# Self-attention's mean squares of the heads' outputs: from ScalarE, head by head, to GpSimd, token tile by token tile

## The chip, the cores and the metric

The kernel runs on one core of one Trainium2 chip. The metric is the time of one execution on the device in microseconds, the median of several runs; lower is better.

## The reference

One decoder layer for 1024 tokens of width 1024, in float32. Ahead of the change stands an input projection and a Mamba-2 mixer; the change is in differential attention, four heads of 128 outputs each:

```python
    p = jax.nn.softmax(s, axis=-1)
    attn = p[:, :, 0] - lam * p[:, :, 1]
    return jnp.einsum('bhqk,bhkv->bhqv', attn.astype(v.dtype), v)
...
    o = rms_norm(o, subln_w) * (1.0 - lambda_init)     # mean of o*o over the 128 outputs of a head
```

Behind it come the output projection, cross-attention into 256 memory tokens, and an MLP. What the change concerns is, for every token and head, the sum of the squares of the 128 outputs `o`, from which `rms_norm` takes its scale.

## The kernel before, in words

All engines run programs of their own, written out in order, and meet at semaphores; each engine works strictly through its own order. Float32 products are made as three products of high and low parts on TensorE (`three`), so most matrices are split: ScalarE makes the high part (`split_hi`, `tr_hi`), VectorE the low part (`split_lo`, `tr_lo`).

**Attention** runs over 32 steps, one for each pair of a query tile i (128 tokens) and a head h. Their order is `ATT_STEPS` (line 183): query tiles in pairs, 7 and 3, 6 and 2, 5 and 1, 4 and 0, the four heads of a pair alternating between its two tiles; tile i has (i + 1) * 128 keys. In step n the engines do, each at its own place in its loop:

- TensorE: two score matrices (L2277, with the mask L2281), the transposes of the combined probabilities of an earlier step (L2296), the product with the values of step n - 3 (L2315) into PSUM bank 7. That product waits for `o_ev` of the step before it, since the bank must be free.
- VectorE: the two maxima (`attn_max`, L1609), and between them the combination of the two softmaxes of step n - 1 (`attn_comb`, L1618, L1619, L1621); `attn_comb` waits for `o_ev` of four steps ago before it overwrites the reciprocals.
- ScalarE: the copy of the transposed probabilities (L1003), the output of step n - 3 taken from PSUM twice, once as a scaled copy into `mix` (L1018) and once as a scaled square with its sum in `stat` (L1023), and the two exponentials (L986).
- GpSimd: next to nothing; it makes the powers of -1/2 for all norms of the kernel, one for each entry of `POWS` (line 199), in that order (`pow_step`, L752).

For the norm of a tile VectorE first scales the four sums to means (`o_mean`, L1626, its instruction is in the helper `mean`, L1338), GpSimd raises them to -1/2, and VectorE multiplies `mix` by the result (`o_norm`, L1631). In VectorE's loop of 39 iterations the mean of a tile stands at the end of the iteration six after the step of its last head (`O_STEP`), the multiplication in the iteration after that, ahead of the mean of the pair's other tile:

```python
                if n - 7 in O_COMPLETE:
                    o_norm(O_COMPLETE[n - 7])
                if n - 6 in O_COMPLETE:
                    o_mean(O_COMPLETE[n - 6])
```

ScalarE copies the last head of that tile in the iteration three after its step. `MIX_TILES` (line 194) is the order in which tiles are complete: 7, 3, 6, 2, 5, 1, 4, 0. In iterations beyond 32 VectorE makes the low parts of the memory tokens, and the means and multiplications of tiles 4 and 0.

**Behind attention** TensorE makes the memory's keys and values in 16 steps (line 2327), two for each unit of weights. The weights pass through two slots: SyncE loads a raw half when the half two before it is split (`load_half` waits for `w_lo`), ScalarE makes its high part (L820), VectorE its low part (L1334), and TensorE waits for both halves' low parts at the first step of a unit (`unit_ready`). After every second step TensorE transposes one tile of `mix` (L2139). In VectorE's order the first of these low parts stand behind the multiplication of tile 0.

Of the kernel before, what the change touches and what calls it, by code (L numbers as in the profile page):

```python
# [27 lines left out]
ALU = mybir.AluOpType  # L28
ACT = mybir.ActivationFunctionType
AX = mybir.AxisListType  # L30

P = 128
T = 1024
D = 1024
NT = T // P
# [6 lines left out]
DH = 4  # L42
# [169 lines left out]
COL, N_COLS = {}, 0  # L212
# [7 lines left out]
def build(nc, t, out):  # L220
    ctx = ExitStack()
    with ctx:
# [10 lines left out]
        def at(name, region, offset, shape, dt=F32):  # L233
            return nc.alloc_sbuf_tensor_at(name, shape, dt, offset=place[region] + offset)
# [9 lines left out]
        def sem(name):  # L244
            return ctx.enter_context(nc.semaphore(name))
# [39 lines left out]
        m_in = at("m_in", "OPL", 0, [P, 2, D])  # L285
        h_mem = at("h_mem", "OPL", 8192, [P, 2, D])
        m_junk = at("m_junk", "OPL", 16384, [P, D])
        kmt = at("kmt", "V", 0, [P, KD, MEM])
        vm = at("vm", "V", 8192, [P, MT, D])

# [129 lines left out]
        ex_done = [sem(f"ex_done{c}") for c in range(2)]  # L420
        comb_done, pt_done, pt_ev, pv_done, o_ev = (sem(n) for n in ("comb_done", "pt_done", "pt_ev", "pv_done", "o_ev"))
        resid_loaded = sem("resid_loaded")
        part_done, sum_done, resid_done, gain_c_loaded = sem("part_done"), sem("sum_done"), sem("resid_done"), sem("gain_c_loaded")
        km_hi, km_lo, qc_hi, qc_lo = sem("km_hi"), sem("km_lo"), sem("qc_hi"), sem("qc_lo")
        ms_done, mmx_done, mex_done, mn_done = sem("ms_done"), sem("mmx_done"), sem("mex_done"), sem("mn_done")
        mt_done, mt_ev, mo_done, mo_hi, mo_lo = (sem(n) for n in ("mt_done", "mt_ev", "mo_done", "mo_hi", "mo_lo"))
# [289 lines left out]
        def _(pool):  # L716
# [54 lines left out]
            def gain_last(j):  # L771

                pool.wait_ge(dn_kept, DN_KEPT["c22"] + j + 1)
                g.tensor_tensor(c22_d[:, j, :], c22_d[:, j, :], gain_a[:, 512:1024], ALU.mult).then_inc(c22_p, 1)

            for what in POWS:
                if what == ("down", 0):
                    for j in range(4):
                        second_half_sum(j, 0)
                        second_half_sum(j, 1)  # L780
                        second_half_rest(j, 0)
                        second_half_rest(j, 1)
                if what == ("down", 4):
                    pool.wait_ge(gain_p_loaded, 16)
                    for j in range(4):
                        gain_last(j)
                pow_step(what)
# [5 lines left out]
        def _(act):  # L793
# [212 lines left out]
            for n in range(NS + 3):  # L1006
                if n >= 2 and n - 2 < NS:
                    probs_evac(n - 2, 0)
                if n == NS + 1:
                    mem_hi(0)  # L1010
                if n == NS + 2:
                    mem_hi(1)
                if n >= 3:
                    k = n - 3
                    i, h = steps[k]
                    act.wait_ge(pv_done, k + 1)
                    o = ps[:, 7, 0:P]
                    s.activation(mix[:, 4 + h, i * P:(i + 1) * P], o, ACT.Copy, scale=recs[:, k % 4, 0:1])  # L1018
                    if k >= 4:
                        act.wait_ge(o_ev, k - 3)  # L1020
                    elif k == 0:
                        act.wait_ge(sq_done, 2 * NT)
                    s.activation(junk[:, (k % 4) * P:(k % 4 + 1) * P], o, ACT.Square, scale=recs[:, k % 4, 0:1],  # L1023
                                 accum_out=stat[:, COL[("o", i)] + h:COL[("o", i)] + h + 1]).then_inc(o_ev, 1)
                if n >= 2 and n - 2 < NS and steps[n - 2][0] >= 4:
                    probs_evac(n - 2, 1)
                if n < NS:
                    attn_exp(n, 0)
                    attn_exp(n, 1)
                if n in (6, 7):  # L1030
                    act.wait_ge(x_loaded[n - 6], 16 * 3)
                    square(("mem", n - 6), m_in[:, n - 6, :], m_junk[:])
# [282 lines left out]
        def _(dve):  # L1315
# [306 lines left out]
                                       probs[:, n % 2, 0, 0:keys], ALU.mult, ALU.add).then_inc(comb_done, 1)  # L1622

            def o_mean(i):
                dve.wait_ge(o_ev, O_STEP[i] + 1)
                mean(("o", i), P, DH)  # L1626

            def o_norm(i):
# [912 lines left out]
```

## Time and profile before

| | |
|---|---|
| median of 3 runs | 1477.35 us (1476.12 to 1478.0) |
| span of the profiled execution, first to last instruction | 1475.4 us |
| its own time as measured without the profiler | not given; the span lies 0.7 us under the lowest run |
| granted TensorE clock, mean | 0.997 of full speed |
| TensorE busy | 1443.8 us, 98% |
| VectorE busy | 934.8 us, 63% |
| ScalarE busy | 685.1 us, 46% |
| GpSimd busy | 86.8 us, 6% |

Busy time is the sum of an engine's instruction records and a share of the whole span; an engine that is busy half of the span can be full in one stage. In the rows, PE is TensorE's products, DVE is VectorE, ACT ScalarE, POOL GpSimd; a number with an L is a line of the kernel, and times are counted from the span's start.

### The profile page before, as it was taken

The page shows a single profiled execution, that of the slowest core. Times are in us where ns is not written, and L with a number is a line of the kernel's source. Part 1 is how long each engine was busy: PE and PEld are TensorE (multiplying, and loading weights), DVE is VectorE, ACT ScalarE, POOL GpSimd, SP SyncE. Part 2 cuts the span into 40 slices and gives each one's busy share as a digit, 9 for nine tenths or more (in the row PEclk, how much of TensorE's full clock was granted, in tenths as well). Part 3 has the DMA queues.
Part 4 walks back from the last instruction along what each step waited for, and adds up shares of the span by engine and source line. Part 5 has one row for each costly group of instructions (what it writes and reads, how often), then busy time and mean ns, then how long its engine had stood idle before and what let it go on. Part 6 is the DMA issues. An engine that isn't in the chain of part 4 may idle for free.

```text
span 1475.4 us, 21355 instructions
## 1 busy us (share of the span) xinstructions
PE 1443.8 (98%) x8008; PEld 1231.0 (83%) x8016; DVE 934.8 (63%) x1586; ACT 685.1 (46%) x1401; POOL 86.8 (6%) x132
## 2 busy tenths in 40 slices
PE   9999999999999999999999999999999999999998
PEld 7889999996669988888988787888888788888886
DVE  4873566737885524523623788887776575557898
ACT  6324222337885423523632565454454464454443
POOL 1000000000010001000000360000000000000011
PEclk9999999999999999999999999999999999999999
DMA  8211111112003621110012343664443697766463
GB/s 317 59 30 57 30 30 30 31 43 72 1 2 109 221 71 30 58 57 30 2 58 71 115 136 114 207 195 176 150 155 116 235 336 268 267 221 193 158 228 129
DMA packets 95381, 177.23 MB, mean 120 GB/s; under 512 B 9904, under 2 KB 34480, under 8 KB 93232
## 3 DMA queue, kind: packets, MB, share of 16 engines
q1 hardware_dynamic: 90384, 153.30, 30.6%
q10 hardware_dynamic: 4896, 22.58, 4.8%
q8 instruction: 64, 1.05, 0.3%
q14 instruction: 37, 0.30, 0.1%
HBM read 138.10 MB, written 37.75 MB: 119 GB/s over the span
## 4 chain that ended last, share of the span: by engine, by line
PE 66%; DVE 4%; issue 2%; ACT 2%; POOL 0%; POOLq 0%; DVEq 0%; ACTq 0%
PE ps L2083 20%; PE ps L2085 20%; PE ps L2084 20%; PE ps L2397 2%; PE ps L2139 1%; DVE nmax L1609 1%; DVE wq_l L1836 1%; ACT probs L986 0%; PE ps L2421 0%; PE ps L2315 0%; PE ps L2408 0%; PE ps L2277 0%; PE ps L2296 0%; ACT probs_t L1003 0%; DVE u_s L1883 0%
## 5 line engine op out<-in xcount | busy, mean ns | idle before, releaser
L2083 PE MATMUL ps<-wh,oph 128*128 128x256 f32 (+2 forms) x768 | 249.0, 324 | 0.0
L2084 PE MATMUL ps<-wl,oph 128*128 128x256 f32 (+2 forms) x768 | 244.9, 319 | 0.0
L2085 PE MATMUL ps<-wh,opl 128*128 128x256 f32 (+2 forms) x768 | 244.9, 319 | 0.0
L2083 PE MATMUL ps<-d_ring 128*128 128x512 f32 x448 | 175.1, 391 | 2.1 <-DVE d_ring L1957 2.1
L2085 PE MATMUL ps<-d_ring 128*128 128x512 f32 x448 | 175.1, 391 | 0.0
L2084 PE MATMUL ps<-d_ring 128*128 128x512 f32 x448 | 175.0, 391 | 0.0
L2085 PEld LDWEIGHTS ps<-wh,opl 128*128 128x128 f32 x768 | 145.1, 189 | 10.9
L2084 PEld LDWEIGHTS ps<-wl,oph 128*128 128x128 f32 x768 | 145.2, 189 | 10.5
L2083 PEld LDWEIGHTS ps<-wh,oph 128*128 128x128 f32 x768 | 145.0, 189 | 10.6 <-ACT vt L947 0.2
L752 POOL TENSOR_TENSOR rms<-stat,mhalf 128x1 f32<-128x1 f32 (+2 forms) x59 | 50.5, 860 | 1339.1 <-DVE stat L1338 1317.4
L1256 ACT ACTIVATE d_ring<-left_raw 128x512 fp32r<-128x512 f32 x112 | 70.4, 629 | 96.0 <-PE ps L2085 73.8
L1951 DVE TENSOR_TENSOR d_ring<-left_raw,d_ring 128x512 fp32r<-128x512 f32 x112 | 78.3, 699 | 54.7 <-ACT d_ring L1256 54.5
L2083 PE MATMUL ps<-oph,wh 128*128 128x512 f32 x256 | 101.2, 395 | 1.4 <-DVE opl L1365 0.9
L2083 PE MATMUL ps<-oph,wq_h 128*128 128x512 f32 x256 | 100.2, 391 | 1.5 <-DVE u_s L1883 1.5
L2083 PEld LDWEIGHTS ps<-d_ring 128*128 128x128 f32 x448 | 84.5, 189 | 20.2 <-issue 2.5
L2085 PE MATMUL ps<-oph,wl 128*128 128x512 f32 x256 | 100.4, 392 | 0.0
L2084 PE MATMUL ps<-opl,wh 128*128 128x512 f32 x256 | 100.3, 392 | 0.0
L2084 PE MATMUL ps<-opl,wq_h 128*128 128x512 f32 x256 | 99.9, 390 | 0.0
L2085 PE MATMUL ps<-oph,wq_l 128*128 128x512 f32 x256 | 99.8, 390 | 0.0
L2085 PEld LDWEIGHTS ps<-d_ring 128*128 128x128 f32 x448 | 84.5, 189 | 17.6
L2084 PEld LDWEIGHTS ps<-d_ring 128*128 128x128 f32 x448 | 84.6, 189 | 17.6
L1334 DVE TENSOR_TENSOR wl<-raw,wh 128x1024 fp32r<-128x1024 f32 (+1 forms) x44 | 53.4, 1224 | 59.8 <-ACT wh L820 59.2
(354 smaller groups left out, 2948.5 us busy)
## 6 DMA issues: line engine op xcount, KB each, us to landing
right_raw<-in_w_down_dram SPq DMA_DIRECT2D x128, 256.0 KB, 3.9
u_kept_s<-us SPq DMA_DIRECT2D x64, 256.0 KB, 2.5
left_raw<-u_kept_s SPq DMA_DIRECT2D x64, 256.0 KB, 3.0
w_blk<-in_w_up_blocks_dram ACTq DMA_DIRECT2D x14, 1024.0 KB, 5.9
left_raw<-u_kept_a SPq DMA_DIRECT2D x48, 256.0 KB, 3.0
raw<-in_w_in_dram SPq DMA_DIRECT2D x16, 512.0 KB, 3.7
u_kept_a<-u SPq DMA_DIRECT2D x24, 256.0 KB, 2.4
x_in<-in_x_dram SPq DMA_DIRECT2D x8, 512.0 KB, 9.2
```

Of the source, the lines that this page charges most:

```text
L752: g.tensor_tensor(dst, src, mhalf[:, 0:w], ALU.pow).then_inc(rms_ready, 1)
L1256: s.activation(d_ring[m % DRING][:, 0, :], left_raw[:, m % 4, :], ACT.Copy).then_inc(dn_hi, 1)
L1334: v.tensor_tensor(wl[:, slot, part], raw[:, q % 2, n], wh[:, slot, part].bitcast(F32), ALU.subtract).then_inc(w_lo, 1)
L1609: v.tensor_reduce(nmax[:, n % 2, c:c + 1], src[:, 0:keys], AX.X, ALU.max, negate=True).then_inc(mx_done[c], 1)
L1836: v.tensor_tensor(wq_l[:, n % RING], src, wq_h[:, n % RING].bitcast(F32), ALU.subtract).then_inc(wq_lo, 1)
L1951: v.tensor_tensor(ring[:, 1, :], left_raw[:, m % 4, :], ring[:, 0, :].bitcast(F32), ALU.subtract).then_inc(dn_lo, 1)
L2083: te.matmul(o, lh, rh, start=first, stop=False)
L2084: te.matmul(o, lh, rl, start=False, stop=False)
L2085: return te.matmul(o, ll, rh, start=False, stop=last)
L2139: ins = te.transpose(ps[:, tr_bank(n) + b, k * P:(k + 1) * P], src(4 * b + k), ident[:])
L2397: ins = te.matmul(ps[:, 6 + d // 4, (d % 4) * P:(d % 4 + 1) * P], vm[:, m, d * P:(d + 1) * P], mprobs_t[:, k % 2, (d // 2) * MT + m, :], s ...
```

## The change

ScalarE makes only the scaled copy of each head's output, and that copy now raises `o_ev`. GpSimd, ahead of each of the eight powers of attention, waits for the copy of the tile's last head, multiplies the tile's 128 x (4 x 128) part of `mix` with itself into a buffer `o_sq`, and adds the halves of each head's 128 squares seven times, 128 values to 64 and so on to one; every one of these eight instructions waits for the one before it on the semaphore `o_squared`. The last writes the four sums into `stat`, where ScalarE's had been. VectorE's `o_mean` waits for the eighth instruction of its tile in place of the copy of the last head. The buffer lies in a region that attention does not use otherwise.

```diff
--- before.py
+++ after.py
@@ -285,6 +285,7 @@
         m_in = at("m_in", "OPL", 0, [P, 2, D])
         h_mem = at("h_mem", "OPL", 8192, [P, 2, D])
         m_junk = at("m_junk", "OPL", 16384, [P, D])
+        o_sq = at("o_sq", "OPL", 20480, [P, DH, P])
         kmt = at("kmt", "V", 0, [P, KD, MEM])
         vm = at("vm", "V", 8192, [P, MT, D])
 
@@ -420,7 +421,7 @@
         ex_done = [sem(f"ex_done{c}") for c in range(2)]
         comb_done, pt_done, pt_ev, pv_done, o_ev = (sem(n) for n in ("comb_done", "pt_done", "pt_ev", "pv_done", "o_ev"))
         resid_loaded = sem("resid_loaded")
-        part_done, sum_done, resid_done, gain_c_loaded = sem("part_done"), sem("sum_done"), sem("resid_done"), sem("gain_c_loaded")
+        part_done, o_squared, resid_done, gain_c_loaded = sem("part_done"), sem("o_squared"), sem("resid_done"), sem("gain_c_loaded")
         km_hi, km_lo, qc_hi, qc_lo = sem("km_hi"), sem("km_lo"), sem("qc_hi"), sem("qc_lo")
         ms_done, mmx_done, mex_done, mn_done = sem("ms_done"), sem("mmx_done"), sem("mex_done"), sem("mn_done")
         mt_done, mt_ev, mo_done, mo_hi, mo_lo = (sem(n) for n in ("mt_done", "mt_ev", "mo_done", "mo_hi", "mo_lo"))
@@ -773,7 +774,24 @@
                 pool.wait_ge(dn_kept, DN_KEPT["c22"] + j + 1)
                 g.tensor_tensor(c22_d[:, j, :], c22_d[:, j, :], gain_a[:, 512:1024], ALU.mult).then_inc(c22_p, 1)
 
+            def squares_of_o(i):
+
+                pool.wait_ge(o_ev, O_STEP[i] + 1)
+                o = mix[:, 4:8, i * P:(i + 1) * P]
+                n = 8 * MIX_TILES.index(i)
+                if n:
+                    pool.wait_ge(o_squared, n)
+                g.tensor_tensor(o_sq[:], o, o, ALU.mult).then_inc(o_squared, 1)
+                for w in (64, 32, 16, 8, 4, 2):
+                    n += 1
+                    pool.wait_ge(o_squared, n)
+                    g.tensor_tensor(o_sq[:, :, 0:w], o_sq[:, :, 0:w], o_sq[:, :, w:2 * w], ALU.add).then_inc(o_squared, 1)
+                pool.wait_ge(o_squared, n + 1)
+                g.tensor_tensor(stat[:, COL[("o", i)]:COL[("o", i)] + DH], o_sq[:, :, 0], o_sq[:, :, 1], ALU.add).then_inc(o_squared, 1)
+
             for what in POWS:
+                if what[0] == "o":
+                    squares_of_o(what[1])
                 if what == ("down", 0):
                     for j in range(4):
                         second_half_sum(j, 0)
@@ -1015,13 +1033,7 @@
                     i, h = steps[k]
                     act.wait_ge(pv_done, k + 1)
                     o = ps[:, 7, 0:P]
-                    s.activation(mix[:, 4 + h, i * P:(i + 1) * P], o, ACT.Copy, scale=recs[:, k % 4, 0:1])
-                    if k >= 4:
-                        act.wait_ge(o_ev, k - 3)
-                    elif k == 0:
-                        act.wait_ge(sq_done, 2 * NT)
-                    s.activation(junk[:, (k % 4) * P:(k % 4 + 1) * P], o, ACT.Square, scale=recs[:, k % 4, 0:1],
-                                 accum_out=stat[:, COL[("o", i)] + h:COL[("o", i)] + h + 1]).then_inc(o_ev, 1)
+                    s.activation(mix[:, 4 + h, i * P:(i + 1) * P], o, ACT.Copy, scale=recs[:, k % 4, 0:1]).then_inc(o_ev, 1)
                 if n >= 2 and n - 2 < NS and steps[n - 2][0] >= 4:
                     probs_evac(n - 2, 1)
                 if n < NS:
@@ -1622,7 +1634,7 @@
                                        probs[:, n % 2, 0, 0:keys], ALU.mult, ALU.add).then_inc(comb_done, 1)
 
             def o_mean(i):
-                dve.wait_ge(o_ev, O_STEP[i] + 1)
+                dve.wait_ge(o_squared, 8 * MIX_TILES.index(i) + 8)
                 mean(("o", i), P, DH)
 
             def o_norm(i):
```

## Rows read from the trace of the kernel before

**Rows 1.** The page of the kernel before, busy time by engine

```profile
PE 1443.8 (98%) x8008; PEld 1231.0 (83%) x8016; DVE 934.8 (63%) x1586; ACT 685.1 (46%) x1401; POOL 86.8 (6%) x132
```

**Rows 2.** A stretch; busy us (count) of PE, PEld, DVE, ACT, POOL; PEclk; DMA share, GB/s

```profile
370.00:400.00 30.00, 26.79 (x190) 18.94 (x190) 25.61 (x49) 25.32 (x72) 3.08 (x4) 1.00 0.01 2
```

**Rows 3.** Chain of waits, 335 to 470 us: shares by line, and pieces

```profile
by line: issue 12.4%; DVE nmax L1609 8.2%; ACT probs L986 5.4%; PE ps L2315 4.6%; PE ps L2083 4.2%; PE ps L2277 4.1%; PE ps L2084 4.0%; PE ps L2085 4.0%; PE ps L2296 3.5%; PE ps L2139 2.6%; ACT probs_t L1003 2.4%; ACT junk L1023 2.0%; DVE r
...
392.50 0.99 DVE nmax L1609
...
415.27 0.45 ACT junk L1023 x2
...
449.35 0.35 ACT junk L1023 x2
...
450.80 0.50 ACT junk L1023 x2
```

**Rows 4.** Groups by line, 340 to 452 us: the squares

```profile
L1023 ACT ACTIVATE junk<-ps,recs 128x128 f32<-128x128 f32 x32 | 11.9, 371 | 0.0
```

**Rows 5.** GpSimd, forms (busy us, mean ns), then L774 and L752 (ns min/median/max)

```profile
L743 POOL MEMSET inv<- 128x1 f32 x32 | 1.1, 99 | 0.0
L740 POOL TENSOR_SCALAR_AFFINE_SELECT mask_s<-mask_s 128x512 bf16<-128x512 bf16 x1 | 0.6, 637 | 0.0
...
L738 POOL TENSOR_SCALAR_AFFINE_SELECT mask_q<-mask_q 128x128 bf16<-128x128 bf16 x1 | 0.3, 295 | 0.0
L722 POOL TENSOR_SCALAR_AFFINE_SELECT ident<-ident 128x128 f32<-128x128 f32 x1 | 0.3, 294 | 0.2 <-POOL mhalf L720 0.2
...
L774 POOL TENSOR_TENSOR c_d<-c_d,gain_a x4: 1293/1296/1797, 1434.6 to 1444.2; 128x512 f32<-128x512 f32 x4
...
L752 POOL TENSOR_TENSOR rms<-stat,mhalf x59: 539/546/1816, 35.9 to 1470.3; 128x1 f32<-128x1 f32 x50, 128x4 f32<-128x4 f32 x8, 128x8 f32<-128x8 f32 x1
```

**Rows 6.** VectorE instructions with two SBUF inputs: L1836 beside GpSimd, L1621 in attention

```profile
L1836 DVE TENSOR_TENSOR wq_l<-w_blk,wq_h x44: 680/684/1782, 833.0 to 1146.7; 128x512 fp32r<-128x512 f32 x44
...
390.21 1.15 DVE L1621 SCALAR_TENSOR_TENSOR probs<-probs,ratio 128x896 f32<-128x896 f32 x1
```

**Rows 7.** Timeline of GpSimd (start us, us): the powers of tiles 7, 6 and 5

```profile
388.49 1.01 POOL L752 TENSOR_TENSOR rms<-stat,mhalf 128x4 f32<-128x4 f32 x1 [15.44 <-DVE stat L1338]
...
413.73 1.01 POOL L752 TENSOR_TENSOR rms<-stat,mhalf 128x4 f32<-128x4 f32 x1 [20.13 <-DVE stat L1338]
...
435.78 1.01 POOL L752 TENSOR_TENSOR rms<-stat,mhalf 128x4 f32<-128x4 f32 x1 [17.38 <-DVE stat L1338]
```

**Rows 8.** Timeline of VectorE: the means of tiles 3, 2 and 1

```profile
392.34 0.16 DVE L1338 TENSOR_SCALAR stat<-stat 128x4 f32<-128x4 f32 x1
...
417.15 0.16 DVE L1338 TENSOR_SCALAR stat<-stat 128x4 f32<-128x4 f32 x1
...
438.93 0.16 DVE L1338 TENSOR_SCALAR stat<-stat 128x4 f32<-128x4 f32 x1
```

**Rows 9.** Busy time and granted clock (PEclk) at the stage's end

```profile
442.00:444.00 2.00, 0.37 (x4) 0.33 (x4) 1.54 (x5) 1.46 (x9) 0.00 (x0) 1.00 0.00 0
...
446.00:448.00 2.00, 2.00 (x11) 2.00 (x11) 0.00 (x0) 0.49 (x2) 0.00 (x0) 0.50 0.01 4
```

**Rows 10.** Timelines of ScalarE, VectorE and TensorE behind attention

```profile
448.98 0.37 ACT L1018 ACTIVATE mix<-ps,recs 128x128 f32<-128x128 f32 x1 [0.22 <-PE ps L2315]
...
454.60 0.69 DVE L1631 TENSOR_TENSOR mix<-mix,rms 128x512 f32<-128x512 f32 x1 [1.12 <-POOL rms L752]
455.21 2.35 DVE L1334 TENSOR_TENSOR wl<-raw,wh 128x1024 fp32r<-128x1024 f32 x2
...
463.47 1.23 DVE L1334 TENSOR_TENSOR wl<-raw,wh 128x1024 fp32r<-128x1024 f32 x1 [1.17 <-ACT wh L820]
...
458.28 0.36 PE L2083 MATMUL ps<-memh,wh 128*128 128x256 f32 x1
...
464.91 0.36 PE L2083 MATMUL ps<-memh,wh 128*128 128x256 f32 x1
```

## The prediction

> **What bounds the kernel now.** I read the page first: TensorE is busy 98% of the span [rows 1], so a change pays or costs only where TensorE waits. The change touches one stage, differential attention, at 340 to 452 us. By stretches [rows 2] ScalarE is there busy 25.3 of 30 us and VectorE 25.6 of 30, both near full and bound to each other step by step. The third view is the chain of waits: it passes from VectorE's maxima to ScalarE's exponentials, TensorE and back. Two things are to be seen in it. The squares that the change removes (L1023) have 2.0% of a stretch of 135 us, that is 2.7 us [rows 3]; and the maximum at 392.50, the first instruction behind tile 3's mean on VectorE, lies on it [rows 3]. The last views are the timelines of VectorE, GpSimd and the end of the stage, for when each mean is due and when GpSimd can begin.
>
> **Removed: 32 squares on ScalarE.** One is 371 ns [rows 4], and with its accumulator read some 0.35 us in sequence; 32 are 11 us of ScalarE, the most that could come back. But only what lies on the chain counts, since without the squares the rest of that chain is still there. The chain shown begins at 382 and has 2.7 us of them for 24 squares; the eight earlier ones, at the same density, 0.9. Not all of it is kept: the 0.45 at 415.27 falls into an interval that the new wait sets (below), and the 0.35 and 0.50 at the end [rows 3] lie behind the last copies and are covered by the longer end. Left: 2.7 + 0.9 - 1.3 = 2.3 us gained. The copy now gives the signal, so TensorE's next product and VectorE's reuse of the reciprocals are released earlier; that is the same gain, not a second one.
>
> **Added: eight chains on GpSimd.** For each token tile one product of 512 elements and seven additions of 256, 128, 64, 32, 16, 8 and 4, each waiting for the one before: 1,020 elements in 8 instructions. A GpSimd product of 512 takes 1.29 us undisturbed [rows 5]. The trace has no small addition there, so its fixed part has to be bounded. The two mask selections, 637 ns for 512 elements and 295 ns for 128 [rows 5], give 0.89 ns per element and 0.18 us fixed, and they read and write as an addition does: that is the nearest row. Below, a memset of one element is 99 ns (1.1 us for 32, the same row group); above, a power of one element is 0.54 us [rows 5]. With 0.18 fixed, the sum is 8 x 0.18 + 1,020 x (1.29 - 0.18) / 512 = 3.65 us (3.2 with 0.10, 5.8 with 0.54). Between two dependent GpSimd instructions the trace shows 0.2 us once [rows 5], and from VectorE's signal to GpSimd's start 0.1; I take 0.15 for each of 8: 1.2. A chain is 4.85 us (3.8 to 7.4).
>
> The Trainium skill (GPSIMD Engine Reference, section on performance versus the Vector engine) speaks against the change: it calls VectorE about twice as fast for two-input elementwise work. It gives 4497 ns for 2048 elements, nearly no fixed part; by that, an estimate, the eight instructions take 2.7 us in place of 3.65, a chain 3.9 us, and the change costs about 5 us less than I forecast.
>
> **Neighbours on the port.** The trace shows GpSimd and VectorE hold each other up: a VectorE subtraction with both inputs in SBUF is 0.68 us in the median and 1.78 at most, the long ones standing beside GpSimd's products, which themselves grow from 1.29 to 1.80 [rows 5, 6]. In attention the VectorE instruction of that kind is the combination of the probabilities (L1621), 1.15 us at 390.21 [rows 6]. It waits for the product and then keeps the first addition waiting.
>
> **Where the chains fall.** Tiles come in pairs, 7 and 3, 6 and 2, 5 and 1, 4 and 0. The first of a pair has time: its mean stands in VectorE's order three steps behind the copy of its last head, and 32 steps take 112 us, 3.5 each. The second has not. GpSimd works in the order squares, power, squares, power, so the squares of tile 3 can begin only behind tile 7's power, which waits for tile 7's mean. That power ends at 389.50 (388.49 + 1.01) [rows 7], while tile 3's mean is due at 392.34 [rows 8], 2.8 us later. The chain needs 0.1 + 4.85 + 1.15 (behind L1621) = 6.1: ready at 395.6, a stall of 3.2 us. Likewise tile 2: from 414.74 to 420.7, due at 417.15, 3.6 us; tile 1: from 436.79, with 0.9 for the port, to 442.6, due at 438.93, 3.7 us [rows 7, 8]. VectorE stands at the mean, and queued behind it are the next maximum and the next combination; ScalarE's exponentials and TensorE wait for those. Nothing covers this, as the maximum behind is on the chain, and VectorE has little idle time there to win it back. Sum: 10.5 us. The power of the second tile stays hidden, its use comes some 3 us later.
>
> The three chains in the shadow (tiles 7, 6, 5) cost nothing by themselves, but can hold a combination for part of a product: 0 to 1.1 us each, I take 0.6 in all, as most of such a delay falls where VectorE waits for ScalarE anyway. TensorE stands in the stalls and may lose its clock. The rows at the stage's end show this happening: after its activity fell away at 442 the granted clock was 0.50, the 1.2 GHz level, in 446 to 448 [rows 9]. I take 0.8 for the three stalls (0 to 4).
>
> **The end of the stage.** Tile 4's last head is copied at 448.98 to 449.35 [rows 10]. Chain to 454.3, mean to 454.5, power (1.01) to 455.6, chain of tile 0 to 460.5, mean to 460.75, power to 461.9, its normalisation (0.69) to 462.6. Only then comes VectorE to the low parts of the weights' next unit, now at 455.21 [rows 10]: 7.4 us later. TensorE has two steps of work in the unit before and then needs these low parts: now they end at 457.56 and its third step begins at 458.28; new end 465.0, so TensorE starts 6.8 us later. Having stood for 6.7 us, it starts at the lower clock; 2.7 us at half speed, about what the end of the stage shows, are 1.3 more: 8.1. The unit behind it depends on VectorE too, through the reload of the raw half (low part from 463.47, TensorE at 464.91 [rows 10], 0.2 us of slack): 7.2 late, less than TensorE itself. From there TensorE bounds, so the delay stays. The end costs 8.1 us.
>
> **Sum.** -2.3 + 10.5 + 0.6 + 0.8 + 8.1 = +17.7 us. The profiled execution has a span of 1475.4; the lowest of three runs is 1476.12 and the median 1477.35, so some 1 to 2 us lie around the span, untouched by the change. On the median: 1495 us.
>
> **Rivals.**
> 1. *The end is hidden*: TensorE and the weight units have more slack than I read, and only the three stalls count: -2.3 + 10.5 + 1.4 = +9.6, 1487 us. For it: VectorE is only half busy behind 455. Against it: the 0.2 us of slack, and nothing can pass the mean in VectorE's queue. Chance 0.12.
> 2. *Small instructions are dear*: a fixed part as in the powers, 0.38 (from 0.54 for one element and 1.01 for four) to 0.54 us. A chain grows by 1.2 to 2.2 us and the total by five times that (three stalls, two chains at the end): +24 to +29, 1501 to 1506 us. For it: only powers are seen at such sizes. Chance 0.15.
> 3. *ScalarE is the bound, and the change is faster*: if the removed 0.35 us came back in each of the 32 steps, 11.2 us, against the shortest chains of 3.8 us without the port, which cost 1.1 + 1.5 + 1.8 in the stalls and 5.1 at the end, 9.5: -1.7, 1475.6 us. The stalls are gone altogether from the point where a power and a chain fit before the second mean, 3.9, 3.4 and 3.2 us after the power's start [rows 7, 8], so with chains under 2.1 us. Against it: VectorE is as busy as ScalarE, and the squares' share of the chain. Chance 0.05.
>
> That the change does not do what it says I exclude: the mean waits for GpSimd's eight instructions by a count.
>
> **How the numbers follow.** The forecast (three stalls and a late end, chains of 4.5 to 5.5 us) has 0.68. Its own range is 1490 to 1499. To leave out no more than 2 in 10 the range takes in rival 1 and the lower part of rival 2: 1484 to 1504. What a measurement can tell from no change is 0.2%, 3 us: only rival 3 reaches there or below. Slower 0.95, same 0.03, faster 0.02.
>
> **What would show it.** GpSimd: 64 new instructions, 29 us by durations of 3.65 a tile, more with the port. VectorE: idle time before the means L1338, released by GpSimd, three times about 3 us and twice more at the end; longer combinations beside GpSimd's. TensorE: one gap of 6 to 7 us before the third step behind attention, with a granted clock of 0.5 after it. ScalarE: the 11.9 us of L1023's squares [rows 4] and their reads gone. Wrong would be the forecast if the means of tiles 3, 2 and 1 found GpSimd done, if a small addition took under 0.1 or over 0.4 us, or if the gap behind attention were under 3 us.

## The result and the profile after

The changed kernel takes 1496.31 us in the median of four runs (1496.18 to 1498.31), beside 1477.13 us (1476.12 to 1478.0) of the kernel before on the same chip: a ratio of 1.0135 [1.0122, 1.0148], 19 us slower. The forecast was 1495.0. (The times of one kernel fall into two groups: of 21 executions of the kernel before, beside run 1, eight lie at 1475.5 to 1476.3, eleven at 1477.2 to 1478.2 and two between, so terms of 1 to 2 us are read from the traces, and one trace is one execution.) The profiled execution has a span of 1494.6 us and took 1496.35 by its own time, so 1.75 us lie around the span; against the span of before it is 19.2 us longer. The page of the changed kernel:

```profile
span 1494.6 us, 21370 instructions
...
PE 1452.4 (97%) x8016; PEld 1237.8 (83%) x8016; DVE 940.3 (63%) x1586; ACT 674.9 (45%) x1337; POOL 120.8 (8%) x196
```

Against [rows 1] ScalarE is busy 10.2 us less, with 64 instructions fewer, and GpSimd 34.0 us more with 64 more; VectorE is busy 5.5 us more with the same 1586 instructions, some of which take longer beside GpSimd's (below). TensorE's products, the same in both kernels, take 8.6 us longer, and its mean granted clock is 0.991 in place of 0.997. The stretches show where (columns as in [rows 2]):

```profile
370.00:400.00 30.00, 24.75 (x163) 16.94 (x162) 23.45 (x41) 19.29 (x46) 13.47 (x20) 0.94 0.00 1
...
382.00:384.00 2.00, 2.00 (x15) 2.00 (x14) 1.25 (x3) 1.24 (x3) 0.00 (x0) 0.72 0.00 0
384.00:386.00 2.00, 2.00 (x8) 1.26 (x8) 1.93 (x4) 1.17 (x4) 0.00 (x0) 0.50 0.00 0
...
474.00:476.00 2.00, 2.00 (x11) 2.00 (x11) 0.65 (x2) 0.18 (x1) 0.00 (x0) 0.50 0.93 274
```

In 370 to 400 us VectorE and ScalarE, near full before [rows 2], are now at 23.45 and 19.29 of 30: both wait more, and ScalarE also has its squares no longer. Behind waits of TensorE (2.0 us up to 381.78, and 5.1 up to 473.60) the granted clock is at 0.50, the 1.2 GHz level, in 384 to 386 and in 474 to 476.

**VectorE.** Its timeline, the instructions of the normalisation and of the weights:

```profile
376.44 3.26 DVE L1366 SCALAR_TENSOR_TENSOR h_mem<-m_in,rms,gain_b 128x1024 f32<-128x1024 f32 x2
...
396.90 0.17 DVE L1350 TENSOR_SCALAR stat<-stat 128x4 f32<-128x4 f32 x1 [1.41 <-POOL stat L790]
...
424.21 0.17 DVE L1350 TENSOR_SCALAR stat<-stat 128x4 f32<-128x4 f32 x1 [1.41 <-POOL stat L790]
...
448.86 0.17 DVE L1350 TENSOR_SCALAR stat<-stat 128x4 f32<-128x4 f32 x1 [1.40 <-POOL stat L790]
...
463.59 0.17 DVE L1350 TENSOR_SCALAR stat<-stat 128x4 f32<-128x4 f32 x1 [2.11 <-POOL stat L790]
...
469.19 0.17 DVE L1350 TENSOR_SCALAR stat<-stat 128x4 f32<-128x4 f32 x1 [2.77 <-POOL stat L790]
...
471.10 2.35 DVE L1346 TENSOR_TENSOR wl<-raw,wh 128x1024 fp32r<-128x1024 f32 x2
```

The means of tiles 3, 2 and 1 [rows 8] each wait 1.4 us for GpSimd, and the two at the end 2.1 and 2.8. The low parts of the weights start at 471.10 in place of 455.21 [rows 10].

**GpSimd.** Its forms, first (busy us, mean ns), then its timeline about tiles 3 and 4:

```profile
L784 POOL TENSOR_TENSOR o_sq<-mix 128x512 f32<-128x512 f32 x8 | 9.7, 1206 | 30.9 <-ACT mix L1036 30.9
...
L788 POOL TENSOR_TENSOR o_sq<-o_sq 128x256 f32<-128x256 f32 x8 | 7.0, 875 | 0.6
...
L788 POOL TENSOR_TENSOR o_sq<-o_sq 128x32 f32<-128x32 f32 x8 | 2.0, 255 | 0.6
...
L790 POOL TENSOR_TENSOR stat<-o_sq 128x4 f32<-128x4 f32 x8 | 1.8, 226 | 0.6
```

```profile
390.64 1.02 POOL L753 TENSOR_TENSOR rms<-stat,mhalf 128x4 f32<-128x4 f32 x1 [8.85 <-DVE stat L1350]
391.63 1.04 POOL L784 TENSOR_TENSOR o_sq<-mix 128x512 f32<-128x512 f32 x1
392.75 3.83 POOL L788 TENSOR_TENSOR o_sq<-o_sq 128x256 f32<-128x256 f32 x6
396.66 0.20 POOL L790 TENSOR_TENSOR stat<-o_sq 128x4 f32<-128x4 f32 x1
...
459.58 1.04 POOL L784 TENSOR_TENSOR o_sq<-mix 128x512 f32<-128x512 f32 x1 [9.45 <-ACT mix L1036]
460.69 2.59 POOL L788 TENSOR_TENSOR o_sq<-o_sq 128x256 f32<-128x256 f32 x6
463.36 0.20 POOL L790 TENSOR_TENSOR stat<-o_sq 128x4 f32<-128x4 f32 x1
```

Tile 4's chain takes 4.0 us (459.58 to 463.56). VectorE works beside it too, but on low parts that have only one input in SBUF (L1359), and no instruction of either engine is longer for it. Tile 3's begins directly behind tile 7's power, as forecast, and takes 5.2 (391.63 to 396.86), since VectorE's combination stands beside it, which itself takes 1.70 us in place of 1.15. The chain of waits about tile 4 goes from ScalarE's copy through GpSimd alone:

```profile
459.16 0.34 ACT mix L1036
459.58 1.05 POOL o_sq L784
460.69 0.73 POOL o_sq L788
...
463.36 0.20 POOL stat L790
```

**TensorE** behind attention, the first transposes of `mix`, the third step of the keys, and the second transposes:

```profile
467.46 1.04 PE L2151 MATMUL ps<-ident,mix 128*128 128x128 f32 x8
...
473.60 0.55 PE L2095 MATMUL ps<-memh,wh 128*128 128x256 f32 x1 [5.09 <-DVE wl L1346]
...
481.56 1.04 PE L2151 MATMUL ps<-ident,mix 128*128 128x128 f32 x8
```

**Where the 19.2 us are.** ScalarE's 32 copies of heads' outputs, one a step, are the same instruction in both kernels; how much later the k-th starts than before is the delay gathered so far. It is +0.20 at the first, -0.12 at the seventh and eighth, +2.02 at the eleventh, +4.57 at the 13th, +4.49 at the 19th, +7.07 at the 21st, +7.27 at the 27th, +10.44 at the 29th. TensorE's first transposes of `mix` (before at 457.49) are +9.97, the third step (before at 458.28 [rows 10]) +15.32, and the second transposes (before at 464.12) +17.44; GpSimd's power that stands at 561.7 before is +17.6. The last 1.6 come near 864, where TensorE waits 2.1 us in both kernels and only in the changed one's profile the clock falls. Before:

```profile
844.00:848.00 4.00, 2.33 (x15) 2.07 (x16) 3.34 (x5) 1.15 (x2) 1.36 (x2) 1.00 0.43 174
848.00:852.00 4.00, 4.00 (x19) 3.32 (x18) 2.24 (x4) 3.15 (x7) 2.08 (x2) 1.00 0.56 184
```

and after:

```profile
860.00:864.00 4.00, 1.90 (x12) 1.36 (x11) 3.31 (x7) 2.30 (x4) 2.46 (x3) 1.00 0.61 251
864.00:868.00 4.00, 4.00 (x14) 3.27 (x13) 2.85 (x5) 1.52 (x3) 0.64 (x2) 0.57 0.22 88
```

So: squares -0.3; tile 7's chain +2.1; three stalls 2.55 + 2.6 + 3.2 = +8.3; the end of the stage +7.5, less 0.5 between the last stall and the first transposes, where the kernel before lost its clock too [rows 9]; small rests +0.5 (0.2 of them stand already at the first copy, before the change acts, and 0.2 come between the 24th and the 26th); the clock near 864 +1.6. The end's 7.5 are 5.35 up to the third step, where TensorE waits, and 2.1 between there and the second transposes, where it works at 0.50.

### The profile page after: what moved, and what is told of

Its sections match the earlier page's. It is cut to its first block, busy times and chain, and to the rows that moved or that the text cites. A ratio compares the mean times of both kernels' runs of the same rounds, so it can differ in the third digit from the quotient of the medians.

```text
span 1494.6 us, 21370 instructions
## 1 busy us (share of the span) xinstructions
PE 1452.4 (97%) x8016; PEld 1237.8 (83%) x8016; DVE 940.3 (63%) x1586; ACT 674.9 (45%) x1337; POOL 120.8 (8%) x196
## 4 chain that ended last, share of the span: by engine, by line
PE 64%; DVE 3%; issue 1%; ACT 1%; POOL 1%; POOLq 0%; DVEq 0%; ACTq 0%
PE ps L2095 20%; PE ps L2097 20%; PE ps L2096 20%; PE ps L2409 2%; PE ps L2151 1%; DVE wq_l L1848 1%; PE ps L2433 0%; PE ps L2420 0%; POOL o_sq L788 0%; DVE u_s L1895 0%; POOL rms L753 0%; DVE h_tok L1787 0%; POOL t3l L770 0%; DVE wl L1346 0%; POOL o_sq L784 0%
## 5 line engine op out<-in xcount | busy, mean ns | idle before, releaser
L2096 PEld LDWEIGHTS ps<-wl,oph 128*128 128x128 f32 x768 | 145.2, 189 | 10.5
L2095 PEld LDWEIGHTS ps<-d_ring 128*128 128x128 f32 x448 | 84.5, 189 | 20.1 <-issue 2.5
```

The source lines that it names most:

```text
L2095: te.matmul(o, lh, rh, start=first, stop=False)
L2096: te.matmul(o, lh, rl, start=False, stop=False)
```

## The experiments

The theories, as the expectations name them: theory A is the ledger above, term by term; rival B is for each run the other reading named with it. Delays are again those of ScalarE's copies against before, unless another instruction is named.

**1. The squares alone.** The changed kernel without chains: the entries of `stat` for `o` are set once to 128 by a memset, and the means wait for the copy. The scale of the heads' outputs is left out of the result.

```diff
...
-                if what[0] == "o":
-                    squares_of_o(what[1])
...
-                dve.wait_ge(o_squared, 8 * MIX_TILES.index(i) + 8)
+                dve.wait_ge(o_ev, O_STEP[i] + 1)
```

> The changed kernel without GpSimd's chains: ScalarE makes no squares, nobody else does, and the means of attention are scaled from a constant set once at the start (the sums of squares of the heads' outputs are left out). What is measured is the worth of the 32 removed squares alone. Theory A, from the two traces: the squares lay beside other work, since the copies of the changed kernel gain only 0.3 us on those of before over the first eight steps; so 1476.3 to 1477, that is 0.2 to 0.8 us under before. Rival B, my prediction's term: the squares on the chain of waits come back, 2.3 us or, with the last two at the end, up to 3.6 us: 1473.5 to 1474.8. Rival C: ScalarE bounds the stage, 11 us: 1466.

Measured: 1475.75 us (1474.82 to 1477.15, 11 runs) beside 1477.19 (21 runs), a ratio of 0.9993 [0.9984, 1.0002]. Its page:

```profile
PE 1444.6 (98%) x8008; PEld 1232.4 (84%) x8016; DVE 934.5 (63%) x1586; ACT 674.5 (46%) x1337; POOL 86.8 (6%) x133
```

ScalarE is busy 10.6 us less, and the first transposes come at 456.98, 0.51 us earlier. The delay goes from +0.08 to -0.23 in the first seven steps and to no more than -0.35 in the 24 behind them. The median lies between the ranges of theory A and rival B, and its ratio alone (1.0 us, from 2.4 gained to 0.3 lost) excludes neither. The trace decides for A: taking all squares away is worth 0.5 us there, and that is about the most that any version of this idea could gain.

**2. Three chains that nobody waits for.** The kernel before, its squares kept, and for tiles 7, 6 and 5 the same eight GpSimd instructions into a buffer that nobody reads.

```diff
+            for what in POWS:
+                if what[0] == "o" and what[1] in (7, 6, 5):
+                    idle_chain(what[1])
```

> The kernel before, with ScalarE's squares kept and used, and GpSimd making the chains of eight instructions for tiles 7, 6 and 5 into a buffer that nobody reads; no other engine waits for them. Nothing is left out. Theory A: what the changed kernel lost between steps 7 and 9 (2.3 us) is the port shared with VectorE, where tile 7's chain meets the two normalisations of the memory rows, and a TensorE clock that falls in the gap this makes; tiles 6 and 5 cost nothing. So about 1479.0 (1478.5 to 1480), and VectorE's L1354 grows from 1.28 us to about 1.65. Rival B: the loss came from the moved signal or the missing squares, and GpSimd's reads are free for others: 1477.1, L1354 unchanged. Rival C: every chain costs VectorE a held combination, 3 x 1.1 us: 1480.4.

Measured: 1478.63 us (1476.94 to 1480.6, 11 runs), 1.0015 [1.0006, 1.0023]. VectorE's pair of normalisations of the memory tokens, in the kernel before and here beside tile 7's chain, and the stretch behind it:

```profile
376.55 2.48 DVE L1354 SCALAR_TENSOR_TENSOR h_mem<-m_in,rms,gain_b 128x1024 f32<-128x1024 f32 x2
```

```profile
376.69 3.26 DVE L1370 SCALAR_TENSOR_TENSOR h_mem<-m_in,rms,gain_b 128x1024 f32<-128x1024 f32 x2
```

```profile
384.00:386.00 2.00, 2.00 (x9) 1.26 (x10) 1.72 (x4) 1.46 (x7) 0.00 (x0) 0.50 0.00 0
```

The pair takes 3.26 us in place of 2.48, and the clock, 1.00 there before, falls to 0.50. The delay is +0.13 up to the eighth copy, +2.41 at the tenth, and +2.27 from the eleventh to the 24th: all of that is tile 7's, and tile 6's chain adds nothing. Behind tile 5's it rises to +2.50 by the 26th. The changed kernel has the same 3.26 and the same fall. The profiled execution took 1480.37 us, 1.7 over this run's median, so in most executions the three chains cost less than in this trace.

**3. The chains of tiles 6 and 5 only.** As run 2, with `in (6, 5)`.

> The kernel before, with chains on GpSimd that nobody reads for tiles 6 and 5 only. Theory A (of the three such chains only tile 7's costs, because it falls beside the normalisation of the memory tokens on VectorE): no difference, 1477.2 us (1476.5 to 1478), copies of all heads within 0.3 us of before. Rival B (every chain holds VectorE up): two thirds of 1.5 to 2.3 us, 1478.2 to 1478.8.

Measured: 1476.63 us (1476.22 to 1478.3, 11 runs) beside 1476.31 (21 runs), 1.0001 [0.9992, 1.0010]; no copy up to the 24th is more than 0.03 us off, and those from the 26th to the 31st are +0.20, so tile 5's chain costs 0.2 us. A chain in the shadow, meeting only the combinations, is nearly free.

**4. Memsets in place of tile 7's chain.** The kernel before, and at tile 7 eight memsets over the same areas, each waiting for the one before.

```diff
-                g.tensor_tensor(o_sq[:], o, o, ALU.mult).then_inc(o_squared, 1)
+                g.memset(o_sq[:], 1.0).then_inc(o_squared, 1)
...
-                    g.tensor_tensor(o_sq[:, :, 0:w], o_sq[:, :, 0:w], o_sq[:, :, w:2 * w], ALU.add).then_inc(o_squared, 1)
+                    g.memset(o_sq[:, :, 0:2 * w], 1.0).then_inc(o_squared, 1)
```

> The kernel before, with eight memsets on GpSimd in place of a chain, for tile 7 alone, over the same areas of the same buffer (512, 128, 64 ... elements), each waiting for the one before: GpSimd is busy at the same place but reads nothing. Theory A (the delay at tile 7 comes from GpSimd's reading SBUF beside VectorE's normalisation of the memory tokens): no delay, copies within 0.3 us of before, the pair of normalisations 2.5 us long, 1477.2 us. Rival B (that GpSimd is busy at all, or writes, is enough): the pair grows toward 3.3 us and the copies are 1 to 2.3 us later.

Measured: 1476.36 us (1474.97 to 1477.98, 11 runs), 1.0001 [0.9992, 1.0010]. GpSimd's timeline, then VectorE's:

```profile
376.59 0.52 POOL L784 MEMSET o_sq<- 128x512 f32 x1 [2.92 <-ACT junk L1039]
377.18 1.88 POOL L788 MEMSET o_sq<- 128x512 f32 x7
```

```profile
377.18 2.47 DVE L1370 SCALAR_TENSOR_TENSOR h_mem<-m_in,rms,gain_b 128x1024 f32<-128x1024 f32 x2
```

The seven later memsets run inside the pair, and the pair keeps its 2.47 us; the delay is +0.63 to +0.64 from the first copy to the 30th, so it was there before the memsets and they add nothing. The memsets are shorter than the chain (2.5 us against 6), but they cover the first normalisation and half of the second, and in the changed kernel both had grown, from 1.28 us to between 1.60 and 1.75. GpSimd's writing does no harm there; the chain that also reads does. The Trainium skill (SBUF — State Buffer, section "Who interferes with whom") says that a VectorE instruction with two SBUF inputs contends with a GpSimd instruction that reads SBUF, and not with one that only writes it. Runs 2 and 4 agree: 3.26 us beside the reads, 2.47 beside the writes.

**5. Both tiles' squares ahead of both powers.** The order in GpSimd's queue becomes squares 7, squares 3, power 7, power 3.

```diff
-                if what[0] == "o":
-                    squares_of_o(what[1])
+                if what[0] == "o" and MIX_TILES.index(what[1]) % 2 == 0:
+                    squares_of_o(what[1])
+                    squares_of_o(MIX_TILES[MIX_TILES.index(what[1]) + 1])
```

> The changed kernel with GpSimd's order turned round within a pair: both tiles' squares first, then both powers. Nothing is left out. Theory A: the three stalls of VectorE at the means of tiles 3, 2 and 1 (8.1 us in the trace) come from the order squares, power, squares and go entirely; at the end tile 0's chain starts one mean and one power earlier, but tile 4's power then waits for it: 0.3 to 1 us less. 1496.3 - 8.1 - 0.6 = 1487.6 (1486 to 1489), a little more if the second chain now meets VectorE's combinations. Rival B: GpSimd's throughput and the port bound the stage whatever the order: 1494 to 1497.

Measured: 1488.0 us (1487.32 to 1488.54, 4 runs), 1.0075 [1.0061, 1.0089], 8.3 us less than the change. GpSimd's timeline, then VectorE's mean of tile 3, then TensorE:

```profile
381.76 1.04 POOL L784 TENSOR_TENSOR o_sq<-mix 128x512 f32<-128x512 f32 x1
...
389.08 1.02 POOL L753 TENSOR_TENSOR rms<-stat,mhalf 128x4 f32<-128x4 f32 x1 [2.62 <-DVE stat L1351]
393.23 1.01 POOL L753 TENSOR_TENSOR rms<-stat,mhalf 128x4 f32<-128x4 f32 x1 [3.12 <-DVE stat L1351]
```

```profile
392.99 0.16 DVE L1351 TENSOR_SCALAR stat<-stat 128x4 f32<-128x4 f32 x1
```

```profile
458.37 1.03 PE L2152 MATMUL ps<-ident,mix 128*128 128x128 f32 x8
464.64 0.55 PE L2096 MATMUL ps<-memh,wh 128*128 128x256 f32 x1 [5.23 <-DVE wl L1347]
```

Tile 3's chain starts at 381.76 instead of 391.63, its mean waits for nobody, and the first transposes are +0.88 in place of +9.97. The wait at the end stays. Two things more are seen. The pair of normalisations is as long as in the changed kernel (1668 ns on average against 1670), but here the clock stays at 1.00 from 382 to 388:

```profile
384.00:386.00 2.00, 2.00 (x14) 1.04 (x14) 1.97 (x4) 0.90 (x5) 1.69 (x5) 1.00 0.00 0
```

The delay from the eighth copy to the eleventh is 0.96 us instead of 2.14: of tile 7's 2.1 us about 1.0 is the port and 1.1 the clock. TensorE's wait just ahead is the same in both, 2.02 us in the changed kernel and 2.03 here; why the clock falls behind one and not behind the other stays open. And chains now meet VectorE twice more, +0.6 at the 18th copy and +1.1 at the 26th. At the end of attention the clock stays at 1.00 (446 to 454), where the kernel before loses it [rows 9], which gives back 1.6. So the 8.3 us of the medians, and the 9.0 by which the span is shorter, are the stalls' 8.3 with other terms on both sides.

**6. The end moved later.** The means and multiplications of tiles 4 and 0 leave the last iterations of attention and go behind the weights' low parts in the steps 3, 5 and 7 of the memory's keys and values; `o_sq` gets another free place.

```diff
-                if n - 7 in O_COMPLETE:
+                if n - 7 in O_COMPLETE and n < NS:
...
-                if n - 6 in O_COMPLETE:
+                if n - 6 in O_COMPLETE and n < NS:
...
+                if n == 3:
+                    o_mean(4)
+                if n == 5:
+                    o_norm(4)
+                    o_mean(0)
+                if n == 7:
+                    o_norm(0)
```

> The changed kernel with the means and multiplications of tiles 4 and 0 moved on VectorE from the end of attention into the keys' and values' steps, behind the low parts of the weights (steps 3, 5 and 7 of 16), and the buffer of the squares moved to another free place. Nothing is left out. Theory A: the end of the stage (tile 0's chain in front of the first low parts) costs 7.5 us, and all of it goes: 1488.8 (1487.5 to 1490), and TensorE has no gap before its third step. Rival B, the end is hidden: nothing is won, 1496. Rival C: the clock of TensorE falls anyway at the end of attention and half of the gain is lost: 1492.

Measured: 1488.03 us (1487.07 to 1489.06, 4 runs), 1.0076 [1.0062, 1.0089]. TensorE's transposes:

```profile
467.45 1.04 PE L2158 MATMUL ps<-ident,mix 128*128 128x128 f32 x8
474.08 1.03 PE L2158 MATMUL ps<-ident,mix 128*128 128x128 f32 x8
```

The first are where the changed kernel has them, and the second come 6.6 us later as before the change, not 14.1: the 7.5 us are gone. The span is 9.3 us shorter, since this profile also lacks the fall of the clock near 864 (1.6 us).

**7. The kernel before with the end moved.** The same move without the chains, to see whether it is worth something by itself.

> The kernel before with the means and multiplications of tiles 4 and 0 moved on VectorE behind the low parts of the weights, as in late_end, and nothing of the change. Nothing is left out. A control for late_end. Theory A: there is no chain to wait for in the kernel before and TensorE has no gap at its third step, so the move wins nothing of itself: 1477.2 (within 0.7 us). Rival B: the move is worth something by itself, 1 us or more: 1476 or less.

Measured: 1477.51 us (1475.5 to 1478.31, 10 runs), 1.0000 [0.9991, 1.0009]. No gain in the medians: run 6 takes back a cost of the change. In the trace two accidents of the clock stand against each other: it doesn't fall at the end of attention (1.00 in 446 to 448), and the first transposes come 1.2 us earlier; but it falls behind TensorE's 2.1 us of waiting at 844.62, as in the changed kernel near 864, and that costs 1.6. So that fall comes also without any chain on GpSimd.

**8. Both repairs.** Runs 5 and 6 in one kernel.

> Both orders mended at once: GpSimd makes both tiles' squares before both powers, and VectorE's means and multiplications of tiles 4 and 0 stand behind the low parts of the weights. Nothing is left out. Theory A: the two costs are separate and add: of the stage's 17.5 us only what tile 7's chain costs on the shared port is left (2.3 us, less 0.3 for the squares). 1479.2 (1478.3 to 1481). Rival B: the three stalls hid a part of the end or the other way round, so the two gains of 8.3 us each do not add: 1483 or more. Rival C: with the stalls gone the removed squares show their worth at last, 2 to 4 us: 1475 to 1477.

Measured: 1479.29 us (1477.75 to 1480.84, 11 runs) beside 1477.34 (27 runs), 1.0013 [1.0004, 1.0022]. The gains add up: 1488.0 and 1488.03 each save about 8.3, and both save 17.0. The transposes are +1.14 and the span is 1476.6, 1.2 over before. That this is what tile 7's chain costs alone, as theory A has it, is in part luck: by the copies GpSimd's chains cost three times, 0.94 at tile 7, 0.6 at the 18th copy and 1.2 up to the 26th, 2.7 in all, and 1.6 come back because the clock doesn't fall at the end of attention.

**9. Tile 7's chain held back.** Run 8, and GpSimd waits with that chain until the memory tokens are normalised.

```diff
                 pool.wait_ge(o_ev, O_STEP[i] + 1)
+                if i == 7:
+                    pool.wait_ge(h_ready, MT)
```

> As pair_late, and tile 7's chain on GpSimd waits until VectorE has normalised the two memory rows. Nothing is left out. Theory A: what is left of the cost is that one meeting on the port and the TensorE clock behind it; without it 1477.0 (1476.2 to 1478.2), the time of before, since all 32 squares are worth no more than 1 us. Rival B: the port costs the same wherever the chain stands: 1479 as in pair_late. Rival C: below 1475.5, a version that beats both.

Measured: 1480.02 us (1478.85 to 1480.91, 11 runs), 1.0020 [1.0011, 1.0029]: no gain, theory A was wrong. GpSimd's product now starts at 378.98. What VectorE does beside it:

```profile
380.19 1.04 DVE L1636 SCALAR_TENSOR_TENSOR probs<-probs,ratio 128x384 f32<-128x384 f32 x1
...
384.38 1.70 DVE L1636 SCALAR_TENSOR_TENSOR probs<-probs,ratio 128x896 f32<-128x896 f32 x1
```

The two chains, one behind the other, now meet two combinations, which take 1.04 us (0.62 before) and 1.70 (1.15 before). The delay grows by 1.43 us from the eighth to the eleventh copy, where run 8 has 0.94. The collision was only moved. The rest of the 1.7 us between the two profiled executions is the clock, which is at 0.50 here in 448 to 450 and at 1.00 in run 8.

**10. Chains three additions longer.** The changed kernel, with three more dependent additions of four elements in each chain; the counts of `o_squared` follow, 11 a tile in place of 8.

```diff
+                for w in range(3):
+                    n += 1
+                    pool.wait_ge(o_squared, n)
+                    g.tensor_tensor(o_sq[:, :, 2:3], o_sq[:, :, 2:3], o_sq[:, :, 3:4], ALU.add).then_inc(o_squared, 1)
```

> The changed kernel with three more dependent additions of four elements in each of the eight chains, their result used by nobody. Nothing is left out. One such addition and its gap measured 0.30 us in the changed kernel, so a chain grows by 0.9 us. Theory A: the total grows by five times that, once in each of three stalls and twice at the end: 4.5 us, 1500.8 (1500 to 1502). Rival B: only the three stalls count: 2.7 us, 1499.0. Rival C: only the end counts: 1.8 us, 1498.1.

Measured: 1497.85 us (1497.59 to 1500.82, 4 runs), 1.0147 [1.0131, 1.0162], only 1.5 us over the changed kernel, under all three forecasts and nearest to rival C. The second transposes behind attention, and the wait ahead of them:

```profile
477.07 0.55 PE L2099 MATMUL ps<-memh,wh 128*128 128x256 f32 x1 [6.75 <-DVE wl L1350]
484.22 1.04 PE L2155 MATMUL ps<-ident,mix 128*128 128x128 f32 x8
```

Inside the stage the stalls did grow as theory A has it: by the copies 3.4, 3.4 and 4.35 us in place of 2.55, 2.6 and 3.2, and TensorE's wait 6.75 in place of 5.09. That speaks against both rivals. But at the second transposes the kernel is only 2.7 us behind the changed one, not 4.5: it was 0.5 us ahead at the eleventh copy (0.3 of that from the first copy on), 0.5 came back between the 29th and the 31st copy, and 0.8 behind the third step, which starts 3.5 us later. And it shows no fall of the clock at 864, which the changed kernel's profile has, and that hides 1.6 us. The median could not settle it, so the run was repeated with a term large enough.

**11. Chains twelve additions longer.** As run 10, with `range(12)` and 20 counts a tile.

> The changed kernel, with twelve further dependent additions of four elements in every chain of GpSimd (one is 0.22 us, with the gap before it 0.30), so each chain is 3.6 us longer. The run with three more was disturbed by where TensorE's clock happened to fall, so this one makes the term large against such accidents. Theory A (each chain's length stands on the path five times, three stalls and two chains at the end): + 5 x 3.6 = 18 us over the changed kernel, 1514 us (1511 to 1518); means of tiles 3, 2 and 1 each wait about 3.6 us longer, the second step of transposes behind attention is 18 us later. Rival B (part of a longer chain is absorbed, as VectorE and ScalarE win back a delay in the steps behind): by the run with three more, 1.5 us for 0.9 us of chain, so 6 to 12 us, 1502 to 1508.

Measured: 1513.78 us (1512.9 to 1515.01, 4 runs) beside 1476.31 (21 runs), 1.0251 [1.0237, 1.0265]; by the ratios 17.1 us over the changed kernel. GpSimd, VectorE's mean of tile 3, and TensorE:

```profile
396.79 3.29 POOL L792 TENSOR_TENSOR o_sq<-o_sq 128x4 f32<-128x4 f32 x12
```

```profile
400.38 0.17 DVE L1354 TENSOR_SCALAR stat<-stat 128x4 f32<-128x4 f32 x1 [4.76 <-POOL stat L794]
```

```profile
493.37 0.55 PE L2099 MATMUL ps<-memh,wh 128*128 128x256 f32 x1 [11.77 <-DVE wl L1350]
...
501.64 1.04 PE L2155 MATMUL ps<-ident,mix 128*128 128x128 f32 x8
```

The mean of tile 3 waits 3.35 us longer than in the changed kernel, the second transposes are 20.1 us later, and the span is 18.7 us longer. The twelve additions take 3.36 us (396.79 to 400.15), five times that is 16.8, and the medians grew by 17.1. Rival B (a part is absorbed) falls: each of the five places costs at least the chain's growth. That the sum comes out as five is in part luck. Up to the second transposes it is six: 13.1 us in the stage, where three chains are 10.1, and 7.0 at the end, where two are 6.7. The longer stalls also take the clock, 0.50 in 400 to 406 and in 432 to 434, where the changed kernel keeps 1.00 behind the means of tiles 3 and 2. The 1.4 us between 20.1 and 18.7 are again the clock: from 1180 to 1188 the changed kernel's shows 0.70 and 0.87 (the kernel before has the like from 1160), this one 1.00 at the same work.

## Why the prediction was right, and where it was not

The time was forecast as 1495.0 and is 1496.31. The mechanisms are those forecast: GpSimd's order of squares and powers stalls the second tile of three pairs, and the end of the stage is late by two chains. Runs 5, 6 and 8 show each by taking it away, run 11 its price. But that the sum is within 1.5 us is luck: on the spans +17.7 stands against +19.2, and the terms are off by +2.0 (squares), -2.2 (stalls), +0.7 (first chains and clock), -1.1 (end) and +2.1 (the clock near 864 and small rests, not forecast).

- **Squares removed, -2.3: mis-sized, it is -0.3 in the changed kernel and -0.5 in run 1.** The step that failed is that what lies on the chain of waits comes back in full, taken as 2.7 + 0.9 - 1.3. Run 1 shows that the squares' share of that chain was only an upper bound. The likely reason is that VectorE's path beside it was nearly as long (VectorE busy 25.6 of 30 us, ScalarE 25.3 [rows 2]) and set the time at once; no run shows this by itself.
- **Three stalls, 3.2 + 3.6 + 3.7 = +10.5: they are 8.3.** The chain was sized at 4.85 us without the port, and takes 4.0. The eight operations were nearly right, 3.65 forecast, and 3.4 in tile 4's chain (3.98 us less 0.55 of gaps); the fixed part of 0.18 holds, as 0.20 for four elements shows. The mask selections from which it came [rows 5] read one input in bf16, an addition two in f32, so that it fitted so well is luck too. The gaps were not right: 0.08 us each (0.6 for 8), where the forecast took 0.15, a little under its one row of 0.2 [rows 5]. With the port a chain took 5.2, 5.0 and 4.8 us, where 6.0 had been assumed for the first two. By the rate of the Trainium skill (GPSIMD Engine Reference, section on performance versus the Vector engine) the forecast's text had made a chain 3.9 us, an estimate. The trace comes near it with 4.0, but by two errors that cancel: that estimate has 2.7 us of instructions, with nearly no fixed part, and 1.2 of gaps, and the trace has 3.4 and 0.6 (four elements take 0.20).
- **First chains, +0.6, and clock in the stalls, +0.8: together 1.4; tile 7's chain alone is 2.1.** The text said that such chains can hold a combination, and sized that. It didn't look at what else VectorE does there: the pair of normalisations, two SBUF inputs each, which stood in the trace of before at 376.55. Those cost 1.0 us, and the clock 1.1 behind it. Tile 6 costs nothing and tile 5 0.2 us (run 3). In the stalls of tiles 3 and 2 themselves the clock stays at 1.00, so of the 0.8 forecast there nothing came; it falls behind the third, from 450 to 458.
- **End of the stage, +8.1: it is 7.5, less 0.5 for the clock that before lost there.** TensorE's wait before the third step was forecast as 6.7 us and is 5.1, with chains of 4.0 and 4.3 us (464.83 to 469.15) instead of 4.85. The clock behind it is 0.50, as forecast, but costs 2.1 us (+15.32 at the third step, +17.44 at the second transposes) where 1.3 were forecast.
- **Not forecast: 1.6 us near 864**, far behind the change. TensorE waits there 2.1 us in both kernels; in one profile the clock falls afterwards and in the other it does not. It falls in the profiles of the changed kernel and of runs 5, 7 and 11, and in none of the others; run 7 has no chain on GpSimd, so the chains are not its cause. What decides it was not controlled by any run, and stays open.

Rival 1 (the end is hidden) falls by run 6, where moving it takes 7.5 us away in the trace. Rival 2 (small instructions dear) falls by the row of 226 ns. Rival 3 (ScalarE is the bound) falls by run 1. VectorE's five waits for GpSimd add up to only 9.1 us of idle time, less than the 15.8 us that stalls and end cost: the rest is in longer instructions beside GpSimd's, in waits of later engines and in the clock. At tile 3, VectorE's two instructions ahead of the mean take 0.72 and 1.70 us in place of 0.22 and 1.15 (391.97 and 392.72 in the changed kernel); with the wait of 1.41 that is 2.46 of the 2.55. Idle time ahead of one line is no measure of a stall.

No version tried beats the kernel before. The best, run 8, is 1.0013 [1.0004, 1.0022] of it, and run 1, with no squares at all, is at 0.9993 [0.9984, 1.0002].

## What to carry to other kernels

Before moving work off an engine, measure the kernel without that work: a line's share in the chain of waits only says what it could give if nothing ran beside it, and here 32 squares with a forecast of 2.3 us were worth 0.5. When work goes into an engine's queue between two steps of another chain, write down the queue's order with times: the same instructions cost 8 us in the order squares, power, squares, power. With both squares first that was gone, and 1.7 us came up elsewhere, where two chains then met VectorE. And look up which instructions of the neighbour fall beside the new ones, not only those of the same loop.

## What was not expected of the hardware

- GpSimd's small additions with both inputs in SBUF: 202 ns for 4 elements a partition with nothing in the way (the mean of 226 holds one of 392 beside VectorE, tile 7's), 203 for 8, 221 for 16, 255 for 32, and between two dependent ones 0.08 us. A square (one tensor as both inputs, 512 elements) is 1.04 us undisturbed, where a product of two tensors took 1.29 [rows 5].
- One 0.8 us lengthening of two VectorE instructions cost 0.96 us in run 5 and 2.14 in the changed kernel, since TensorE's clock then fell (0.50 in 384 to 386). TensorE had waited 2.02 us ahead of it in the one and 2.03 in the other. Such falls make terms of 1 to 2 us that come and go between kernels, and an experiment on a term of that size has to be read stretch by stretch, or made larger, as in runs 10 and 11. Larger delays bring falls of their own, as run 11 shows.
- Eight GpSimd memsets beside VectorE's two-input instructions cost those nothing (2.47 us against 2.48), a chain of eight instructions that read SBUF costs 0.8.
